# Seven places of 2 MB for the first layer's expert weights, and expert loops written out

## The reference

```python
def ec_moe(h, w_router, w_e_gate, w_e_up, w_e_down):
    b, t, d = h.shape
    cap = EC_CAPACITY * t // N_EXPERTS
    aff = jax.nn.softmax((h @ w_router).astype(jnp.float32), axis=-1)
    vals, idx = lax.top_k(jnp.swapaxes(aff, 1, 2), cap)
    xs = jax.vmap(lambda hb, ib: hb[ib])(h, idx)
    hid = jax.nn.silu(jnp.einsum('becd,edf->becf', xs, w_e_gate)) * jnp.einsum('becd,edf->becf', xs, w_e_up)
    ys = jnp.einsum('becf,efd->becd', hid, w_e_down) * vals[..., None].astype(h.dtype)
    return jax.vmap(lambda yb, ib: jnp.zeros((t, d), yb.dtype).at[ib.reshape(-1)].add(yb.reshape(-1, d)))(ys, idx)
```

## Time and profile before

| what | us |
|---|---|
| median of 3 runs | 3611.61 |
| span of the profiled execution | 3608.9 |
| PE busy | 3372.9 (93%) |
| PE weight load busy | 2302.5 (64%) |
| DVE busy | 1174.2 (33%) |
| ACT busy | 707.2 (20%) |
| POOL busy | 116.6 (3%) |

### The profile page before, as it was taken

The page is one execution under the profiler, slowest core; times in us unless marked ns, Lnnn a source line. Parts: engine busy times, 40 slices in busy tenths (PEclk is TensorE's granted clock), DMA queues, the critical chain, the costliest instruction groups (busy, mean ns, idle before and its releaser), DMA issues.

```text
span 3608.9 us, 71927 instructions
## 1 busy us (share of the span) xinstructions
PE 3372.9 (93%) x30572; PEld 2302.5 (64%) x30572; DVE 1174.2 (33%) x2567; ACT 707.2 (20%) x1346; POOL 116.6 (3%) x191
## 2 busy tenths in 40 slices
PE   7899999999999899999999989899999999999998
PEld 4456757678764776777677656667677564444544
DVE  1443415346625111111111453425274332222222
ACT  3313321122322000000001432320132201111111
POOL 0000100000000000000000000100000000000000
PEclk9999999999999999999999999999999999999999
DMA  5511120021035899999999401120212269999996
GB/s 226 227 47 59 34 82 13 30 71 46 14 128 220 344 358 352 356 366 373 353 364 365 167 12 62 52 82 13 87 39 76 109 267 416 416 417 419 416 414 289
DMA packets 101983, 738.34 MB, mean 205 GB/s; under 512 B 8272, under 2 KB 14672, under 8 KB 59744
## 3 DMA queue, kind: packets, MB, share of 16 engines
q1 hardware_dynamic: 90512, 692.54, 48.7%
q0 software_dynamic: 11216, 42.00, 4.0%
HBM read 710.34 MB, written 18.92 MB: 202 GB/s over the span
## 4 chain that ended last, share of the span: by engine, by line
PE 73%; DMA 14%; DVE 7%; issue 3%; ACT 3%; DVEq 0%; POOL 0%; SPq 0%; ACTq 0%; POOLq 0%
PE psum L664 14%; PE psum L1265 9%; PE psum L1256 8%; DMA ring<-in_w_e_gate 8%; PE psum L554 8%; PE psum L547 5%; PE psum L1297 5%; PE psum L1117 4%; PE psum L666 3%; DMA ring<-in_w_ada 2%; PE psum L1303 2%; DMA ring<-in_w_e_down 2%; PE psum L531 2%; PE psum L1313 2%; DVE work L2013 2%
## 5 line engine op out<-in xcount | busy, mean ns | idle before, releaser
L664 PE MATMUL psum<-HT,ring 128*128 128x256 f32 x2560 | 599.7, 388 | 13.4 <-DVEq L2266 5.3
L664 PEld LDWEIGHTS psum<-HT,ring 128*128 128x128 f32 x2560 | 488.0, 194 | 98.1 <-issue 21.6
L1265 PE MATMUL psum<-work,ring 128*64 128x96 f32 x11264 | 485.9, 247 | 43.4 <-issue 32.2
L1265 PEld LDWEIGHTS psum<-work,ring 128*64 128x64 f32 x11264 | 471.5, 137 | 59.9 <-issue 49.5
L1496 ACT ACTIVATE work<-psum,small 128x768 f32<-128x768 f32 (+4 forms) x208 | 146.1, 703 | 696.7 <-PE psum L1303 325.6
L554 PE MATMUL psum<-ring,HT 128*128 128x512 f32 (+1 forms) x768 | 276.0, 521 | 0.0
L1256 PE MATMUL psum<-ring,work 128*64 128x256 f32 x1024 | 243.9, 393 | 29.1 <-DMA ring<-in_w_e_gate 28.2
L1257 PE MATMUL psum<-ring,work 128*64 128x256 f32 (+1 forms) x1024 | 238.0, 372 | 0.0
L1499 ACT ACTIVATE work<-psum 128x256 f32<-128x256 f32 (+7 forms) x219 | 103.5, 473 | 652.8 <-PE psum L554 237.8
L1297 PE MATMUL psum<-ring,work 128*64 128x512 f32 x960 | 220.3, 598 | 9.9 <-DMA ring<-in_w_e_down 9.9
L554 PEld LDWEIGHTS psum<-ring,HT 128*128 128x128 f32 x768 | 145.8, 190 | 127.3 <-issue 120.5
(11 more groups left out here) (243 smaller groups left out, 3805.9 us busy)
## 6 DMA issues: line engine op xcount, KB each, us to landing
ring<-in_w_e_gate SPq DMA_DIRECT2D x64, 2048.0 KB, 11.8
ring<-in_w_e_up SPq DMA_DIRECT2D x48, 2048.0 KB, 12.7
ring<-in_w_e_down SPq DMA_DIRECT2D x48, 2048.0 KB, 10.6
ring<-in_w_ada SPq DMA_DIRECT2D x24, 2048.0 KB, 12.4
ring<-in_w_e_up SPq DMA_DIRECT2D x32, 1536.0 KB, 10.2
ring<-in_w_gate SPq DMA_DIRECT2D x16, 2048.0 KB, 8.1
HT<-in_w_e_up SPq DMA_DIRECT2D x16, 2048.0 KB, 23.0
ring<-in_w_e_gate SPq DMA_DIRECT2D x16, 1536.0 KB
```

What stands on the lines that cost most here:

```text
L664: pe.matmul(b[:, 0:256], w[:, k, d4 * P:(d4 + 1) * P], HT[:, k, off:off + 256], start=(k == 0), stop=(k == KD - 1))
L1265: ins = pe.matmul(b[lo:lo + 64, f * cap:(f + 1) * cap], w[:, k, c0:c0 + 64], e_xs[:, k, 0:cap], start=(k == 0), stop=(k == KD - 1))
```

## The change

For both layers a table (`HOMES`, `home_of`) now says where each of the 144 pieces lies. In the first layer the pieces go round seven places of 2 MB in the order of use: `HT` columns 0 to 4096; `HT` 4096 to 6144 together with `YT` 0 to 2048; `YT` 2048 to 6144; `work` 0 to 4096; and the three of the ring. A piece in the second of these is two transfers of half the row each. The last expert leaves out the third place, where the sums of all experts come back. SP waits for the consumer of the piece that lay there before (`used_before`, `consumer`), and each place of each layer has its own semaphore (`w_ht0`, `w_r00` and so on). The first four pieces wait only until the normalised rows are stored, the zeros are written and the router is done; the fifth waits for the first gather (`rows_in`). The transfer of the second layer's packed constants moves behind the first expert's ninth piece. In the second layer the order of the pieces, their places and their waits are those of before. SP's loops and PE's loop of the second layer are written out. A small scratch array, `early_diag[0]`, moves from `work` into `X`.

```diff
+HOMES = [["r0", "r1", "r2", "ht", "ht_yt", "yt", "xn"],
+         ["r0", "r1", "r2", "ht", "xn0", "xn1", "ht_yt"]]
...
+def home_of(L, q):
+    if L == 0:
+        cycle = ["ht", "ht_yt", "yt", "xn"] + [f"r{(N_EXP[0] + i) % SLOTS}" for i in range(SLOTS)]
+        if q < (NE - 1) * PIECES_EXP:
+            return cycle[q % len(cycle)]
+        return [home for home in cycle * 3 if home != "yt"][q - (NE - 1) * PIECES_EXP + (NE - 1) * PIECES_EXP % len(cycle)]
...
+def used_before(L, q):
+    return max((p for p in range(q) if home_of(L, p) == home_of(L, q)), default=None)
...
                     def wpiece(i):
-                        if L == 0:
-                            n = n0 + i
-                            pe.wait_ge(sems[f"w_in{n % SLOTS}"], (e * 3 + (n // SLOTS + 1)) * 16)
...
+                        q = e * PIECES_EXP + i
+                        pe.wait_ge(sems[f"w_{home_of(L, q)}{L}"], expert_landings(L, q))
...
-                if two:
-                    with pe.Fori(0, NE - 1) as e:
-                        c.begin(e, per)
-                        expert(e, False)
-                        c.e = None
-                    c.finish_loop(NE - 1)
-                else:
-                    for e in range(NE - 1):
-                        expert(e, False)
+                for e in range(NE - 1):
+                    expert(e, False)
...
-                with sp.Fori(1, NE) as e:
-                    for i in range(PIECES_EXP):
-                        if L:
-                            freed_place(e, i)
-                        else:
-                            freed(e, i)
-                        piece(e, i)
+                for q in range(PIECES_EXP * NE):
+                    home = home_of(L, q)
+                    before = used_before(L, q)
+                    if L == 0 and q == 0:
+                        sp.wait_ge(sems["aff"], 1)
+                        sp.wait_ge(sems["zeroed"], 16)
+                        sp.wait_ge(sems["xn_stored"], 16 * len(qtiles(0)))
+                    elif L == 0 and q == 4:
+                        sp.wait_ge(sems["rows_in"], 16)
+                    elif L == 0 and q == PIECES_EXP:
+                        sp.dma_start(packs[:, :], I["pack"][1]).then_inc(sems["pack_in"], 16)
...
+                    if before is not None:
+                        read(sp, L, before)
...
+                    for place, k0, k1, width in piece_parts(L, q):
+                        sp.dma_start(place[:, 0:(k1 - k0) * width], weights_of(q // PIECES_EXP, q % PIECES_EXP)[:, k0 * width:k1 * width]
+                                     ).then_inc(sems[f"w_{home}{L}"], 16)
```

More of the change, by code:

```diff
@@ L208, in hybrid_layers @@
                  "sel_rows", "sel_kept", "f_prod", "f_free", "f_zero"] + [f"f_back{t}" for t in range(NT)]
+        names += [f"w_{home}{L}" for L in range(DEPTH) for home in HOMES[L]]
         sems = {n: ctx.enter_context(nc.semaphore(n)) for n in names}
@@ L238, in hybrid_layers, with piece_parts, k_block, expert_landings @@
         w_in = [sems[f"w_in{i}"] for i in range(SLOTS)]
[L240 to L243, removed]
+        ht_ = HT.rearrange("p k t -> p (k t)")
+        PLACE = {"r0": (run(0, SLOT),), "r1": (run(1, SLOT),), "r2": (run(2, SLOT),), "ht": (ht_[:, 0:4096],), "ht_yt": (ht_[:, 4096:6144], YTr[:, 0:2048]), "yt": (YTr[:, 2048:6144],), "xn": (work[:, 0:4096],), "xn0": (work[:, 0:3072],), "xn1": (work[:, 3072:6144],)}
+        def piece_parts(L, q):
+            i = q % PIECES_EXP
+            blocks, width = (KD, EXP_W[i]) if i < 6 else (EXP_DOWN[i - 6], D)
+            place = PLACE[home_of(L, q)]
+            first = blocks if len(place) == 1 else KD // 2 if i < 6 else 2
+            return [(p, k0, k1, width) for p, (k0, k1) in zip(place, ((0, first), (first, blocks)))]
+        def k_block(L, q, k):
+            for place, k0, k1, width in piece_parts(L, q):
+                if k0 <= k < k1:
+                    return place[:, (k - k0) * width:(k - k0 + 1) * width]
+        def expert_landings(L, q):
+            return 16 * sum(len(piece_parts(L, p)) for p in range(q + 1) if home_of(L, p) == home_of(L, q))
         def landings(n):
-            return 16 * (n // SLOTS + 1)
+            return 16 * sum(m <= n and m % SLOTS == n % SLOTS for m in PIECE.values())
         marks = {}
@@ L1287, in down @@
                         kk = EXP_DOWN[i]
-                        w = weight(6 + i, 1024, kk)
-                        split = L > 0 and len(ahead.get(6 + i, ())) == 2
+                        w = weight(6 + i)
                         for k in range(kk):
-                            if split and k == 2:
-                                w = ahead[6 + i][1].rearrange("p (k n) -> p k n", n=1024)
                             f = 4 * i + k
@@ L2956, in need, with read @@
         def need(eng, n):
[L2958 to L2966, removed]
+            name, v = piece_done[n]
+            eng.wait_ge(sems[name], v)
+        def read(eng, L, q):
+            name, v = consumer(L, q)
+            eng.wait_ge(sems[name], v)
         @block.sync
@@ L2978, in stream @@
                 w, src = source(L, name)
-                if n >= SLOTS:
+                if L and n < N_IN[L] + SLOTS:
+                    read(sp, L - 1, max(q for q in range(PIECES_EXP * NE) if home_of(L - 1, q) == f"r{n % SLOTS}"))
+                elif n >= SLOTS:
                     need(sp, n - SLOTS)
@@ L3022, in weights_of @@
                     return I["w_e_down"][L, e, r * D:(r + EXP_DOWN[i - 6] * P) * D].rearrange("(p x) -> p x", p=P)
[L3024 to L3052, removed]
```

65 lines of the change are left out of this document (24 added, 41 removed).

## The result

The changed kernel takes 3618.39 us (median of 20 runs, 3612.37 to 3630.33) against 3611.97 of the kernel before (20 runs): a ratio of 1.0020, interval 1.0012 to 1.0028. It is slower by 6.4 us, a little under what the prediction called no change, and on the side that it did not forecast. Its profiled execution has a span of 3615.1 us, 6.2 more than before.

What follows compares the result with a forecast made beforehand. The prediction took late weights and instruction-fetch stops to bound first-layer experts, DMA the second layer. Span 3608.9 us less 17.5, other terms 0, gave 3591.4; the runs' median lies 2.7 above the span, so 3594, likeliest 3582 to 3604, whole range 3551 to 3629.

Steps and rivals of the forecast that it cites:

- The bound before: First-layer experts, 50.33 us each, lose 3.85 us to waits for weights and stops for PE's program; second layer bound by DMA.
- The floor of 46.48 us an expert: First layer: predicted time of one expert when nothing is late, summed from its matmul stretches.
- Step (1): First-layer experts: pieces waiting for the piece seven before, not three, remove up to all 17.5 us of PE's weight waits.
- Step (2): First-layer experts: instruction stops remain, so loss falls from 3.85 to 2.76 us, 49.2 us an expert; -17.5 us for sixteen.
- that rival: First-layer experts: a stop takes the place of each weight wait, loss stays 3.85 us; 3605 to 3615 us, chance 0.23.
- Step (3): Start of the first layer's experts: four pieces going out before the first gather cost 0, bounds -1 to +3 us.
- Step (5): Second layer's PE loop written out: 0 in the sum, 0 to +2 us; +26 if fetches came late there too.
- Step (6): Seam from the first layer's last expert to the next mixer: 0, and not better than -3.85 us.
- slower: First-layer experts all become like the four with many stops, 51.45 us each; +17 us, 3628, chance 0.20.
- the four slow ones: First-layer experts without weight waits in the earlier trace, 51.45 us on the mean, 1.1 above the average.
- Faster by far: First-layer experts: DMA pauses let fetches start at once, so stops go too; 58 us less, 3554, chance 0.15.

Runs made afterwards that it cites:

- e7_noweights: e2_l1loop without the transfers of the first layer's expert weights after the first seven pieces; 3546.18 us in one run.
- e10_half: e2_l1loop without the transfers of every second piece of the first layer's expert weights after the first seven; 3563.81 us in one run.
- e1_start: The changed kernel, but the first layer's third weight piece and all after it wait for the first gather; 3620.85 us, ratio 1.0023 to the kernel before.
- e11_8k_start: e8_pk8k, but the first layer's third weight piece and all after it wait for the first gather; 3609.22 us, ratio 0.9996.
- e5_l1out: The kernel before, with only PE's second-layer experts written out (three places, SP's loops kept); 3621.71 us, ratio 1.0021.
- e2_l1loop: The changed kernel, but PE's fifteen second-layer experts are a loop again, SP's loops staying written out; 3612.73 us, ratio 0.9994 to the kernel before.
- e6_pk4k: e2_l1loop with each first-layer expert piece sent as four transfers of 4 KB or 3 KB a row; 3606.48 us, ratio 0.9990.
- e8_pk8k: e2_l1loop with each first-layer expert piece sent as two transfers, packets of 8 KB or 6 KB; 3606.56 us, ratio 0.9987.
- e3_l0loop: The kernel before, three places, with PE's fifteen first-layer experts also a loop; 3752.51 us, ratio 1.0376.

## Why the prediction was wrong

**The bound before** was read rightly. The floor of 46.48 us an expert was measured at 45.90 (e7_noweights), and the stops every 256 instructions are waits for PE's program that come with the weights' traffic (e7_noweights, e10_half, and the packets that end just before the stops do). They do not come in gate and up alone: the earlier trace rows leaves out three, 2.7 us, on the choosing lines 1211 and 1215.

**Step (1), depth**, held: the waits for weights went from 17.5 us to none.

**Step (2)** failed, "I take what PE's list leaves when DMA goes". The list's 32.2 us of "issue" did not stay: they became 46.8, 14.6 us more for 17.5 us less. The prediction had written that a stop and a wait "can stand for one another" and gave that rival 0.23; it was the right mechanism. A wait for weights gave the next block time to arrive, and with the wait gone the same block is late. The loss per expert went from 3.85 to 3.5 us over the predicted floor, not to 2.76; and of the forecast 17.5 us the fifteen experts gave 5.3, less than the 6.6 by which two executions of the same code differ (749.7 to 759.5 us in six kernels with seven places, 755.0 and 761.6 with three). The reason given against the rival, that waits stand on top of stops in PE's list, mistook a list of where time was spent for one of causes: each entry is what was left after the others had hidden their part.

**Step (3), the start**, was mis-sized: bounds of -1 to +3 us, measured +8.0 in the changed kernel's profile. Of it 2.5 us are a later issue of the gather, which is not the change's, 3.6 the gather's own length, and 2.0 the lower clock behind PE's longer wait. So the term is 5.5; the medians of a gather amid three-place traffic did not bound one amid four queued pieces. But e1_start and e11_8k_start show that its removal gives nothing back in the time; why is open.

**Step (5), the second layer**, carries the result, and was put at 0. Its bounds, 0 to +2 by bytes, were wrong; the +26 that stood beside them was for fetches that come late to PE, and PE did not wait for them. What was lost is 8.0 us in fourteen experts, 7.4 of them waits of PE for weights (5.0 in e5_l1out), which came later than their bytes and those of the fetches explain. (The 17.7 us a block were worked out from PE's busy time; over the 600 us they are 18.9, and nothing hangs on it.) That "a loop end saved is given to the next wait for weights" was right; that a stage bound by DMA can pay more for packets put among its weights than their bytes, here about six times, was left out. By e2_l1loop and e5_l1out this term is, within their intervals, all of the 6.4 us.

**Step (6)**, the seam, was put at 0, and the stretch from the sixteenth expert to the second layer's second came out 4.6 us shorter. That is not one execution's chance: the stretch takes 998.6 to 1000.9 us in six kernels with seven places (the changed one, e1_start, e2_l1loop, e6_pk4k, e8_pk8k, e11_8k_start) and 1002.6 to 1004.2 in three with three (before, e5_l1out, e3_l0loop). The last expert's down projection is 1.5 to 1.7 us of it, 14.9 us instead of 16.4 to 16.6; where the rest comes from is open. It stands against the later start, and the two may be why the seven places come out even.

Of the rivals, "slower" came near the time (3628 forecast for it), but not by its mechanism: experts of the first layer did not become like the four slow ones on the mean. "Faster by far" fell with its premise that the fetches would find pauses: the engines' share stayed at 0.97 with the weights ahead.

The Trainium skill ("Runtime: NRT & Kernel Launch", Instruction fetch mechanics) says that crossing a block is "mostly hidden": so it is in e7_noweights, at 27 GB/s, and not at 365. It says as well that kernels prefer full unrolling since a taken branch whose target is outside the current window of two pages has to fetch it; the first layer's loop agrees (about 11 us at each end). The second layer's, some 600 instructions and so more than two blocks of 256, does not: it fetched nothing again, and is the faster form by 0.2%.

What stays open: by what rule a fetch and the weights share an engine, since it is not the packets' size; and why 32 fetches cost the second layer about six times their bytes, most of it in a few experts.

## What to carry to other kernels

Before a wait is counted as gain, ask what else happens during it: a fetch of code that it hides comes to light when it goes, and a profile's waits cannot be subtracted one by one. A loop whose code is fetched once cost this DMA-bound stage nothing that shows, and writing it out put packets among its data; a loop too long to be kept pays at each turn. Try a change's parts alone: here one part was neutral in the time and the other, thought to be free, decided the sign.

## What the runs showed of the hardware

- The same PE code runs without a stop at 27 GB/s of DMA traffic, loses 7.6 us to "issue" in the stage at 210, and about 47 at 364.
- A packet of 256 PE instructions takes about 1 us at any of these loads, but begins later: 0.0, 1.7 and 3.8 us after the block before it began (medians; 2.2 with one weight piece under way at a time). PE goes on 1.2 to 1.6 us after the packet ends.
- An indirect gather behind four weight pieces took 11.34 us amid packets of 16 KB and 7.56 amid 4 KB; the stops for program did not follow the packets' size.
- A loop of over 1752 PE instructions stops at each turn, for 6.27 + 4.81 us in the one shown, while its body runs with next to no stops, and TensorE's granted clock is 0.82 in the 12.6 us after (0.98 and more in the straight code's stages).
- A stage at a DMA share of 1.01 fell from 416 to 413 GB/s when 32 packets of 16 KB of program were put into 600 us of it, and took 597.5 us for what had taken 589.5.
